# Prompt attention in half steps of four heads, with a longer pipeline and output ring

## The reference

```python
DILATIONS = ((128, 1), (512, 4), (2048, 16))        # window, dilation; 8 heads x 64
def dilated_band_attention(q, k, v, dil, n_back):   # blocks of 128 queries
    ...                                             # keys: [previous block, own block] of the residue class
    scores = jnp.einsum('znqhd,znkhd->znhqk', qb, kb) * (HEAD_DIM ** -0.5)
    ...
    scores = jnp.where(valid[None, :, None], scores, -jnp.inf)
    lse = jax.nn.logsumexp(scores, axis=-1)
    p = jnp.exp(scores - lse[..., None])
    o = jnp.einsum('znqhk,znkhd->znqhd', p, vb)
def combine_dilations(outs, lses):
    w = jax.nn.softmax(jnp.stack(lses, axis=0), axis=0)
    return jnp.einsum('pbth,pbthd->bthd', w, jnp.stack(outs, axis=0))
```

## Time and profile before

| | us |
|---|---|
| median of three runs | 3184.18 (3178.68 to 3192.13) |
| profiled execution | 3187.13 |
| its span in the trace | 3185.5 |
| PE busy | 2881.9 (90%) |
| PE weight loads | 2395.8 (75%) |
| DVE, ACT, POOL busy | 1351.3, 993.3, 411.8 |
| mean granted TensorE clock | 0.942 |
| prompt attention, from its first load to its last copy | about 493 (680.1 to 1173.3) |

### The profile page before, as it was taken

One profiled execution on the slowest core, in us unless ns is written; L12 is line 12 of the kernel. 1 busy time (PEld: TensorE's weight loads), 2 busy tenths in 40 slices (PEclk: granted clock), 3 DMA queues, 4 the chain that ended last, 5 costly groups with the idle time before them and its releaser, 6 DMA issues. The chain is left out here.

```text
span 3185.5 us, 42658 instructions
## 1 busy us (share of the span) xinstructions
PE 2881.9 (90%) x16437; PEld 2395.8 (75%) x16437; DVE 1351.3 (42%) x2910; ACT 993.3 (31%) x2043; POOL 411.8 (13%) x550
## 2 busy tenths in 40 slices
PE   2899995987888979599959999999999999999998
PEld 1668784766778867388848888888888888899986
DVE  5346763544455533488723332333323332233321
ACT  3112120324555533366612221222212222232210
POOL 1105675420000000000000000000010000100001
PEclk7999998978889979799979999999999999999999
DMA  7563333833333357455466454546435544454421
GB/s 264 166 205 101 120 116 95 288 102 121 107 96 109 104 229 301 169 180 195 163 180 198 145 183 148 171 146 198 152 121 186 185 149 168 154 165 139 146 81 54
DMA packets 335960, 501.88 MB, mean 158 GB/s; under 512 B 23897, under 2 KB 231001, under 8 KB 327066
## 3 DMA queue, kind: packets, MB, share of 16 engines
q1 hardware_dynamic: 316384, 372.41, 36.5%
q0 software_dynamic: 18640, 125.85, 11.3%
q10 hardware_dynamic: 762, 1.21, 0.1%
HBM read 410.11 MB, written 155.95 MB: 178 GB/s over the span
## 5 line engine op out<-in xcount | busy, mean ns | idle before, releaser
L2191 PE MATMUL f_ps_f<-f_h_f,f_ws_f 128*128 128x512 f32 (+1 forms) x5280 | 1003.7, 352 | 27.7 <-DVE f_ws_f L2251 27.7
L2191 PEld LDWEIGHTS f_ps_f<-f_h_f,f_ws_f 128*128 128x128 f32 x5280 | 861.3, 188 | 169.5 <-DVE f_ws_f L2251 27.9
L2209 PE MATMUL f_ps_f<-f_ws_f,f_aT_f 128*128 128x512 f32 x2244 | 519.2, 394 | 1.0 <-DVE f_tmp_f L2261 1.0
L2209 PEld LDWEIGHTS f_ps_f<-f_ws_f,f_aT_f 128*128 128x128 f32 x2244 | 422.4, 188 | 97.0 <-DVE f_tmp_f L2261 1.5
L2251 DVE TENSOR_TENSOR f_ws_f<-f_raw_f,f_ws_f 128x1024 fp32r<-128x1024 f32 x264 | 316.1, 1225 | 417.3 <-ACT f_ws_f L2223 417.3
L2223 ACT ACTIVATE f_ws_f<-f_raw_f 128x1024 fp32r<-128x1024 f32 x264 | 268.5, 1049 | 421.8 <-PE f_ps_f L2209 394.6
L769 PE MATMUL p_out_ps<-p_w,p_hT 128*128 128x512 f32 x1632 | 388.7, 397 | 11.6 <-DVE p_hT L830 8.0
L769 PEld LDWEIGHTS p_out_ps<-p_w,p_hT 128*128 128x128 f32 x1632 | 307.8, 191 | 85.6 <-issue 14.1
L2274 DVE TENSOR_TENSOR f_tmp_f<-f_sl_f,f_ps_f 128x512 f32<-128x512 f32 (+1 forms) x110 | 64.7, 588 | 563.1 <-PE f_ps_f L2191 562.6
L344 PE MATMUL a_o_ps<-a_v,a_probsT 128*128 128x64 f32 x1200 | 175.4, 303 | 71.4 <-DVE a_probsT L399 71.3
L344 PEld LDWEIGHTS a_o_ps<-a_v,a_probsT 128*128 128x128 f32 x1200 | 161.1, 214 | 88.3 <-DVE a_probsT L399 80.4
(11 more groups left out here) (310 smaller groups left out, 2746.3 us busy)
## 6 DMA issues: line engine op xcount, KB each, us to landing
f_raw_f<-in_w_gate_dram SPq DMA_DIRECT2D x88, 512.0 KB, 4.5
f_raw_f<-in_w_up_dram SPq DMA_DIRECT2D x88, 512.0 KB, 5.3
f_raw_f<-in_w_down_dram SPq DMA_DIRECT2D x88, 512.0 KB, 3.9
out_dram<-in_cache_k_dram POOLq DMA_DIRECT2D x8, 4088.0 KB, 14.5
out_dram<-in_cache_v_dram POOLq DMA_DIRECT2D x8, 4088.0 KB, 14.5
p_ring<-in_w_ada_dram SPq DMA_DIRECT2D x32, 512.0 KB, 4.8
b_k<-in_cache_k_dram SPq DMA_DIRECT2D x16, 1024.0 KB
b_v<-in_cache_v_dram SPq DMA_DIRECT2D x16, 1024.0 KB
```

Source lines behind the costliest of these rows:

```text
L2191: mm = pe.matmul(out, ws[:, p % SPLIT, a, k * 128:(k + 1) * 128], h2[:, y, k, c0:c1], start=(k == 0 and x == 0), stop=(k == KT - 1 and x = ...
L2209: mm = pe.matmul(ps[down_bank(b, h, j)][:, :], aT[:, a, k, at:at + 128], ws[:, p % SPLIT, y, (k % 2) * 512:(k % 2 + 1) * 512], start=(k == ...
```

## The change

`attention_stage` is rewritten, with the loops unrolled; the two other edits follow from the sign of the maxima.

- The unit of work is a half step i (four heads): n, quad = divmod(i, 2). PE in half step i does: turn q of step n+2 (odd i) or k of step n+1 (even i); scores of i; turn the probabilities of i-2; values of i-3. Before, probabilities and values were one step (two halves) behind, in one group.
- Where a block has a predecessor and the two lie side by side in `kT` (n % 4 not 0), one product of 256 columns takes the place of two of 128 (24 of the steps).
- The maxima are taken as minima of the scores times -SCALE, in the instruction that adds the mask, and serve as biases as they are: L393 goes. The mask's halves change places.
- Turned rows and turned probabilities share two banks; `o_ps` has two banks; qT three slots; turned probabilities two slots; `o` four slots instead of two, and DVE waits for the store of step n-4.
- SP loads q of step n when q of n-2 is turned, k when k of n-2 is, v when both halves of step n-3 have their values, in this order.
- The mix stage combines minima, with an exponential of scale -1.

```diff
-            def step(n):
-                p, r = n.slot(2), n.slot(4)
-                wait(sp, kT_ps, n.times(1) - 1)
-                sp.dma_start(q[:, p].unsqueeze(1), rows(t["q"], n)).then_inc(qk_loaded[p], 16)
-                sp.dma_start(k[:, p].unsqueeze(1), rows(t["k_prompt"], n)).then_inc(qk_loaded[p], 16)
-                wait(sp, pv_done, n.times(4) - 8)
+            for n in range(STEPS):
+                p, r = n % 2, n % 4
+                if n >= 2:
+                    wait_turned(sp, ("q", n - 2))
+                sp.dma_start(q[:, p].unsqueeze(1), rows(t["q"], n)).then_inc(q_loaded[p], 16)
+                if n >= 2:
+                    wait_turned(sp, ("k", n - 2))
+                sp.dma_start(k[:, p].unsqueeze(1), rows(t["k_prompt"], n)).then_inc(k_loaded[p], 16)
+                if n >= 4:
+                    sp.wait_ge(valued, 2 * (n - 3) + 2)
                 sp.dma_start(v[:, r].unsqueeze(1), rows(t["v_prompt"], n)).then_inc(v_loaded[r], 16)
...
+            def turn_rows(u):
+                kind, n = u
+                src, loaded = (q, q_loaded) if kind == "q" else (k, k_loaded)
+                pe.wait_ge(loaded[n % 2], 16 * (n // 2 + 1))
+                free_turn_bank(u)
...
+            def scores(i):
+                n, quad = divmod(i, 2)
+                wait_out(pe, ("q", n))
+                wait_out(pe, ("k", n))
+                if i >= 2:
+                    pe.wait_ge(masked, i - 1)
...
+                        elif n % 4:
+                            spans = ((0, n % 4 - 1, 2),)
...
+            for u in (("q", 0), ("k", 0), ("q", 1)):
+                turn_rows(u)
+            for i in range(HALVES + 3):
+                n, quad = divmod(i, 2)
+                u = ("q", n + 2) if quad else ("k", n + 1)
+                if u[1] < STEPS:
+                    turn_rows(u)
+                if i < HALVES:
+                    scores(i)
+                if 0 <= i - 2 < HALVES:
+                    probs(i - 2)
+                if 0 <= i - 3 < HALVES:
+                    values(i - 3)
...
+            def exps(i):
...
+                    e = act.activation(pr[:, n % 2, hd, 0:w], pr[:, n % 2, hd, 0:w], ACT.Exp, scale=-1.0, bias=o[:, n % ORING, AW + hd:AW + hd + 1],
...
+                if quad == 0 and n >= ORING:
+                    dve.wait_ge(o_stored[n % 2], 16 * ((n - ORING) // 2 + 1))
+                dve.memset(gate[:, quad:quad + 1], 0.0)
+                for j in range(4):
...
+                                                  -SCALE, 3e38, ALU.add, ALU.min, o[:, n % ORING, AW + hd:AW + hd + 1])
...
+            def o_out(n):
+                dve.wait_ge(valued, 2 * n + 2)
+                dve.tensor_copy(o[:, n % ORING, 0:AW], o_ps[n % 2][:, :]).then_inc(o_sb, 1)
```

More of the change, by code:

```diff
@@ L172, in attention_stage, with units, by_act @@
     STEPS = BLOCKS * len(DILATIONS)
+    HALVES = 2 * STEPS
     SCALE = HD ** -0.5
-    SECTIONS = ((0, 4, False), (4, 16, True), (16, 20, False), (20, 32, True), (32, 36, False),
-                (36, 44, True), (44, 48, False))
-    LOADS = ((0, 4, False), (4, 16, True), (16, 32, True), (32, 48, True))
+    PAIRS = AW // 128
+    ORING = 4
     def has_prev(n):
[L181 to L185, removed]
+        pattern, i = divmod(n, BLOCKS)
+        return i % (BLOCKS // DILATIONS[pattern][1]) > 0
     def rows(a, n):
-        pattern = n.add // BLOCKS
+        pattern, i = divmod(n, BLOCKS)
         d = DILATIONS[pattern][1]
[L191 to L198, removed]
+        z, b = divmod(i, BLOCKS // d)
+        return a[b * QB * d:(b + 1) * QB * d, :].rearrange("(n d) c -> n d c", d=d)[:, z:z + 1, :]
+    def units(i):
+        n, quad = divmod(i, 2)
+        return [(i, 0), (i, 1)] if has_prev(n) else [(i, 0)]
+    turn_order = [("q", 0), ("k", 0), ("q", 1)]
+    for i in range(HALVES + 2):
+        n, quad = divmod(i, 2)
+        turn_order += [x for x in ((("q", n + 2),) if quad else (("k", n + 1),)) if x[1] < STEPS]
+        if i >= 2:
+            turn_order += units(i - 2)
+    turn_index = {u: x for x, u in enumerate(turn_order)}
+    def by_act(u):
+        if u[0] in ("q", "k"):
+            return u[0] == "k"
+        n, quad = divmod(u[0], 2)
+        return u[1] == 0 if has_prev(n) else quad == 0
+    out_count, seen = {}, [0, 0]
+    for u in turn_order:
+        seen[by_act(u)] += 1
+        out_count[u] = seen[by_act(u)]
     with ExitStack() as ctx:
@@ L229, in _ @@
             pool.affine_select(out=mask[:, 0:QB], in_=mask[:, 0:QB], compare_op=ALU.is_ge, fill=NEG,
+                               base=0, pattern=[[1, QB]], channel_multiplier=-1).then_inc(mask_made, 1)
+            pool.affine_select(out=mask[:, QB:], in_=mask[:, QB:], compare_op=ALU.is_ge, fill=NEG,
                                base=0, pattern=[[-1, QB]], channel_multiplier=1).then_inc(mask_made, 1)
[L231 to L238, removed]
+            for n in range(STEPS):
+                pool.wait_ge(o_sb, n + 1)
+                pool.dma_start(rows(t["o"][n // BLOCKS], n), o[:, n % ORING].unsqueeze(1)).then_inc(o_stored[n % 2], 16)
             for p in range(2):
@@ L257, in _ @@
         @block.scalar
         def _(act):
[L259 to L269, removed]
@@ L277, in exps @@
                 e.then_inc(exped, 1)
[L279 to L330, removed]
-                        mm = pe.transpose(p_ps[pair % 2][:, at:at + QB], pr[:, n.slot(2), 2 * pair + x, prev * QB:(prev + 1) * QB],
-                                          const["ident"][:, :])
-                mm.then_inc(pT_ps, 1)
[L335 to L339, removed]
-                for x in range(2):
-                    hd = 2 * pair + x
-                    last = 1 if has_prev(n) else 0
-                    for prev in range(last + 1):
-                        mm = pe.matmul(o_ps[:, hd * HD:(hd + 1) * HD], prT[:, pair % 2, x, prev * QB:(prev + 1) * QB],
-                                       v[:, (n + -prev).add % 4, hd * HD:(hd + 1) * HD], start=(prev == 0), stop=(prev == last))
-                mm.then_inc(pv_done, 1)
-            def step(n):
-                first, last = n.i is None and n.add == 0, n.i is None and n.add == STEPS - 1
-                for quad in range(2):
-                    if not last:
-                        (queries, keys)[quad](n + 1)
-                    if not first:
-                        probs(n + -1, 2 * quad)
-                        probs(n + -1, 2 * quad + 1)
-                    scores(n, quad)
-                    if not first:
-                        values(n + -1, 2 * quad)
-                        values(n + -1, 2 * quad + 1)
-            queries(Turn(0))
-            keys(Turn(0))
-            run_steps(pe, step, SECTIONS, 4)
-            for quad in range(2):
-                for f in (probs, values):
-                    for pair in (2 * quad, 2 * quad + 1):
-                        f(Turn(STEPS - 1), pair)
@@ L369, in _ @@
+            turned_out(act, move, ("k", 0))
+            for i in range(HALVES + 3):
+                n, quad = divmod(i, 2)
+                if quad == 0 and n + 1 < STEPS:
+                    turned_out(act, move, ("k", n + 1))
+                if 0 <= i - 1 < HALVES:
+                    exps(i - 1)
+                if 0 <= i - 2 < HALVES:
+                    for u in units(i - 2):
+                        if by_act(u):
+                            turned_out(act, move, u)
         @block.vector
@@ L403, in outputs_out @@
-            def outputs_out(n):
-                dve.wait_ge(pv_done, n.times(4) + 4)
-                dve.tensor_copy(o[:, n.slot(2), 0:AW], o_ps[:, :]).then_inc(o_sb, 1)
-            def step(n):
-                first, last = n.i is None and n.add == 0, n.i is None and n.add == STEPS - 1
-                if not last:
-                    queries_out(n + 1)
-                for quad in range(2):
-                    if not first:
-                        probs_out(n + -1, 2 * quad)
-                    maxima(n, quad)
-                if not first:
-                    outputs_out(n + -1)
@@ L418, in _ @@
-            queries_out(Turn(0))
-            run_steps(dve, step, SECTIONS, 4)
-            probs_out(Turn(STEPS - 1), 0)
-            probs_out(Turn(STEPS - 1), 2)
-            outputs_out(Turn(STEPS - 1))
+            def o_out(n):
+                dve.wait_ge(valued, 2 * n + 2)
+                dve.tensor_copy(o[:, n % ORING, 0:AW], o_ps[n % 2][:, :]).then_inc(o_sb, 1)
+            dve.wait_ge(mask_made, 3)
+            for n in range(2):
+                turned_out(dve, move, ("q", n))
+            for i in range(HALVES + 3):
+                n, quad = divmod(i, 2)
+                if quad == 1 and n + 2 < STEPS:
+                    turned_out(dve, move, ("q", n + 2))
+                if i < HALVES:
+                    maxima(i)
+                if 0 <= i - 2 < HALVES:
+                    for u in units(i - 2):
+                        if not by_act(u):
+                            turned_out(dve, move, u)
```

(2 more changed lines are left out.)

152 lines of the change are left out of this document (108 added, 44 removed).

## The result

| | before | changed |
|---|---|---|
| median, us | 3188.15 (3178.68 to 3193.44, 4 runs) | 3351.94 (3348.66 to 3359.34, 4 runs) |
| profiled span, us | 3185.5 | 3346.8 |
| prompt attention, first load to last copy | 493.2 | 644.0 |
| mean granted clock, whole kernel | 0.942 | 0.918 |

The changed kernel takes 1.052 times as long (95% interval 1.0487 to 1.0554), 164 us more. The forecast was 3359.

The account below looks back on a forecast made before the run. PE was the busiest engine; the change makes it wait for q loads issued behind v's wait. Start and end 10, work 358 less 5, slow first steps 15, waits 163, clock 127: 668 against 493 us, so 3359 us; range 3265 to 3440.

Parts of the forecast that it names:

- Waits: Prompt attention: PE waits for each q load from step 5 to 47, 43 times 3.8 us, 163 us (138 to 206).
- The estimate of 2.6 us: Landing time of a 256 KB load: about 2 us fixed plus bytes at 436 GB/s; waits would come to 138 us.
- Clock: Prompt attention: after each wait PE runs 6.8 us at half clock, costing 127 us over 43 waits.
- the low and the high row of the forecast: Half-clock stretch after each wait in prompt attention: 3.4 us costs 63 us in all, 10.2 us costs 185.
- Work, start and end: Prompt attention without waits and their clock: 10 us start and end, 353 work, 15 for four slow first steps; 378.
- A step: Prompt attention: a dilation-1 step takes about 15.5 us, a step without a predecessor 12.2.
- Wide scores: Scores of 256 columns in 24 steps of prompt attention save 0.1 us a half, 48 x 0.1 = 5 us.
- Nothing outside the stage moves.: Outside prompt attention: no change, as the sample loads keep about the cover they had, 27 us.
- the fast recovery of the clock: Rival, prompt attention: each wait costs only one 3.4 us half-clock stretch, 64 us less, 3295 us; chance 0.17.
- the stuck clock: Rival, prompt attention: the clock never recovers and stays at 0.50, 3498 us; chance 0.08.
- The working design: Rival, prompt attention: q comes in time, no wait; stage 105 us shorter than now, 3079 us; chance 0.07.
- break-even of 2.7 us: Prompt attention: 115 us over 43 steps; with wait and clock together below 2.7 us a step, the design would win.

Follow-up runs that it names:

- the filled kernel: Changed kernel with 16 unused matmuls of ident by ident on PE ahead of each q wait from step 5 on; 3245.95 us, 1.0198 of the kernel before.
- the kernel with q and k first: Changed kernel with SP issuing q and k of step n+1 ahead of the wait for v of step n; 3055.89 us, 0.960 of the kernel before.

## Why the prediction was right

The mechanism was counted right: one queue in order, v's wait ahead of q's issue, and PE's want of q right behind the work that releases it. The 43 waits, the 0.4 us between the issues (1083.69 to 1084.07), v's issue at the end of the values, and the vanished store waits are all in the profile. Term by term:

- **Waits.** Forecast 163 us (3.8 each). The profile shows 177.6 (4.1), the filled kernel 185. Inside the bounds. The single landing time of 3.2 us stood for two: q landed in 4.3 us in the steps of dilation 4, where the waits were 4.7 to 5.6 us, and in 3.2 to 3.3 in the others, where they were 3.3 to 4.4. The loads of q in the changed kernel, of 850 to 1073 us and of 1085 to 1300 us:

```profile
a_q<-scratch_q SPq DMA_DIRECT2D x15, 256.0 KB, 4.3
...
a_q<-scratch_q SPq DMA_DIRECT2D x14, 256.0 KB, 3.2
```

  The estimate of 2.6 us, with which the waits would have come to 138, rests on a figure that the Trainium skill ("DMA: Bandwidth & Descriptors", the anatomy of one DMA) gives for DMAs issued by GpSimd. These are issued by SP, always behind another load, and the fastest of the changed kernel took 2.9.
- **Clock.** Forecast 127 us, from a stretch of 6.8 us at half clock after each wait. The filled kernel shows 108, the busy times 120. The size was near, the picture behind it was not: few stretches were near 6.8 us. Read in windows of 0.25 us between one wait and the next, PE was at half clock for 3.1 to 4.1 us in 22 of the 43 cases, for 9.5 us or more (up to 13.2) in 11, and for 5.6 us in the mean. Two cases, both in steps without a predecessor (columns as in rows 2):

```profile
746.30:755.80 9.50, 9.50 (x48) 8.27 (x48) 3.24 (x20) 3.62 (x15) 0.00 (x0) 0.50 0.12 46
759.62:763.00 3.38, 3.38 (x18) 2.83 (x19) 1.65 (x11) 0.00 (x0) 0.00 (x0) 0.50 0.24 95
```

  After the first the clock stayed at half into the next wait, after the second it was back at 763.00, and the waits before the two were alike (3.56 and 3.75 us). So the low and the high row of the forecast both came true, each in a part of the steps, and that their mean lay near the middle row was luck. No run here shows what decides between them.
- **Work, start and end.** Forecast 378 us; the kernel with q and k first needs 351. This term was oversized, by 27 us. At full clock a half step without a predecessor takes 2.51 us there (values start at 710.28 and 712.79), where I had taken 2.82 with a wait in it and the old order: 42 x 0.31 = 13 us. One with a predecessor takes 4.26 with wide scores and 4.40 (961.99 to 966.39) with narrow ones, where I had 4.44 less 0.1: about 4 us. The other 10 us are start and end; I took the first four steps at half clock "as now", while the new order had 0.76 to 0.78 there.
- **A step.** Forecast 12.2 us without a predecessor and 15.5 in dilation 1. From one turned q to the next it was 11.9 and 14.9 us in the mean.
- **Wide scores.** Forecast 5 us, measured 3.7 by the medians and some 5 by the stages.
- **"Nothing outside the stage moves."** This step failed. I had given the prefetch "about the cover they had", 27 us. It was issued 39.9 us before the last copy in the kernel before (1133.5) and 18.7 us before it in the changed one (1305.6), since three of the last six half steps have no scores left. And I had not asked what queues behind it. PE began the sample attention 24.6 us after the last copy instead of 9.7, 15 us more; 4.6 us came back in that stage (115.2 against 119.8). The landing of `b_q` follows the prefetch's lead through the kernels that issue it behind: 1.8 us with 39.9 us of lead, 2.8 with 27.3 (five slots of v), 5.6 with 23.8 (before, four slots of o), 12.2 and 13.5 with 18.7 and 18.8.

So the stage took 644 us against the 668 forecast: 27 less work, 22 more wait by the filled kernel, 19 less clock. The 24 us too many there and the net 10 us too few outside it partly cancelled, and the total looks better than its terms.

Of the rivals, the fast recovery of the clock (3295) and the stuck clock (3498) don't hold: the clock cost 108 to 120 us where the first had 63, and the stretches show 0.65 to 0.79 where the second had 0.50, though single steps did as each of them says. The working design (3079) was wrong for this kernel, but the kernel with the queue mended is what it describes, and came in at 3056, 23 us below; its break-even of 2.7 us for wait and clock together stands against (185 + 108) / 43 = 6.8 measured.

## What to carry to other kernels

When the order of the consumer changes, count again for each load between which two pieces of the consumer's work it is issued, and which wait stands ahead of it in its queue; a ring that is deep enough for one tensor can hold back another tensor's load behind it. Price a wait on TensorE with what the clock loses after it: here 43 waits of some 4.2 us cost 178 to 185 us and their clock 108 to 120 more. And try the smallest part of a rewrite alone: two more output slots gave 110 of the 127 us that the whole rewrite could give.

## What the runs showed of the hardware that was not expected

Useless matmuls in place of waiting made the kernel 106 us faster, since the granted clock stayed at 1.00 and the useful work behind each wait ran at full speed.

After waits of about the same length PE ran at half clock for 3.1 us in some steps and for 9.5 us and more in others, within one stage of one kernel.

A load of 64 KB took 12.2 to 13.5 us from issue to landing where it was issued behind a prefetch that kept the DMA engines full, and 1.8 us in the kernel before, where the prefetch had ended. The DMA share (the last column but one) at its issue, at 1336.8 us in the changed kernel, and just ahead of it in the kernel before, issued at 1181.2:

```profile
1337.00:1340.00 3.00, 0.00 (x0) 0.00 (x0) 0.00 (x0) 0.00 (x0) 2.85 (x4) 0.50 1.03 418
```

```profile
1177.00:1181.00 4.00, 0.00 (x0) 0.00 (x0) 0.00 (x0) 0.00 (x0) 0.00 (x0) 0.50 0.00 0
```
